# Two mLSTM/attention layers and a compressed-attention layer: a hand-written order of VectorE and ScalarE work before the head loops

## What is computed

```python
for l in range(2):
    h = rmsnorm(x, norm_mix_g[l])
    q,k (conv + silu), v, o, gates i,f, attention q,k,v, ga, gb = split(h @ w_in[l])
    logf = log_sigmoid(f + b_fgate); ig = i + b_igate       # 4 heads: gate rows
    hm = mlstm(q, k, v, ig, logf)                            # running sum and running max of the rows
    ha = sliding_window_attention(aq, ak, av)                # 16 query heads, 4 key/value heads
    x = x + (sigmoid(ga) * (hm @ wm) + sigmoid(gb) * (ha @ wa)) @ w_out[l]
    x = x + square(relu(rmsnorm(x) @ w_up)) @ w_down
x = rmsnorm(x, final_g)
h = rms_norm(x, pre_gain)
# third layer: k,v of three branches (compressed, selected, full), q, 3 gates per head, z
kc = silu(blocks(k_cmp) @ w1) @ w2; vc likewise               # "x2": tokens of two strides, then "hidden"
x = x + rms_norm(sum over branches(gate * attention) * z @ w_out)
```

## Time and profile before

| | |
|---|---|
| median of 3 runs | 2405.76 us (2405.76 to 2406.56) |
| the profiled execution | 2405.57 us, its span 2403.5 us |
| TensorE busy | 2317.2 us, 96% of the span |
| VectorE, ScalarE, GpSimd busy | 920.9, 972.0, 885.2 us |
| mean granted clock | 0.982 |
| transfers | 193.84 MB, 81 GB/s |

### The profile page before, as it was taken

One profiled execution on the slowest core, in us unless ns is written; L12 is line 12 of the kernel. 1 busy time (PEld: TensorE's weight loads), 2 busy tenths in 40 slices (PEclk: granted clock), 3 DMA queues, 4 the chain that ended last, 5 costly groups with the idle time before them and its releaser, 6 DMA issues.

```text
span 2403.5 us, 35769 instructions
## 1 busy us (share of the span) xinstructions
PE 2317.2 (96%) x11397; PEld 1917.0 (80%) x11397; DVE 920.9 (38%) x1907; ACT 972.0 (40%) x2051; POOL 885.2 (37%) x672
## 2 busy tenths in 40 slices
PE   6999999999999998999999999999999999999996
PEld 4888888788888886888888788888887878888885
DVE  7343343324132136243343324132136335445452
ACT  4455455434232234455455434222234244445443
POOL 3333333444444444333333444444444321221213
PEclk9999999999999999999999999999999999999998
DMA  3221222222222222221222222222223221110202
GB/s 121 70 77 63 87 70 70 79 87 96 97 97 96 96 91 93 70 79 61 87 71 69 79 89 94 97 97 96 96 89 117 104 71 53 44 64 32 70 35 70
DMA packets 58793, 193.84 MB, mean 81 GB/s; under 512 B 6654, under 2 KB 11311, under 8 KB 58352
## 3 DMA queue, kind: packets, MB, share of 16 engines
q1 hardware_dynamic: 50400, 177.48, 21.7%
q10 hardware_dynamic: 8336, 15.60, 1.9%
HBM read 190.89 MB, written 2.16 MB: 80 GB/s over the span
## 4 chain that ended last, share of the span: by engine, by line
PE 89%; DVE 5%; ACT 2%; issue 2%; ACTq 0%; DVEq 0%; POOL 0%; POOLq 0%
PE ps L485 25%; PE ps L487 24%; PE ps L486 24%; PE ps L547 4%; PE ps L527 3%; PE ps L535 2%; PE ps L645 1%; PE ps L501 1%; PE ps L633 1%; PE ps L786 1%; PE ps L748 1%; PE ps L811 1%; DVE sz L1363 0%; DVE tn L1805 0%; ACT e_buf L908 0%
## 5 line engine op out<-in xcount | busy, mean ns | idle before, releaser
L446 POOL TENSOR_TENSOR w_lo<-w_raw,w_hi 128x512 fp32r<-128x512 f32 x664 | 878.6, 1327 | 1497.4 <-ACT w_hi L861 1493.5
L485 PE MATMUL ps<-hT_hi,w_hi 128*128 128x512 f32 x1600 | 653.6, 409 | 0.6 <-DVE qn L1333 0.6
L487 PE MATMUL ps<-hT_hi,w_lo 128*128 128x512 f32 x1600 | 630.9, 394 | 0.0
L486 PE MATMUL ps<-hT_lo,w_hi 128*128 128x512 f32 x1600 | 630.2, 394 | 0.0
L861 ACT ACTIVATE w_hi<-w_raw 128x512 fp32r<-128x512 f32 x664 | 411.3, 626 | 483.3 <-PE ps L487 455.3
L487 PEld LDWEIGHTS ps<-hT_hi,w_lo 128*128 128x128 f32 x1600 | 304.0, 190 | 66.8
L485 PEld LDWEIGHTS ps<-hT_hi,w_hi 128*128 128x128 f32 x1600 | 305.0, 191 | 64.4 <-issue 8.6
L486 PEld LDWEIGHTS ps<-hT_lo,w_hi 128*128 128x128 f32 x1600 | 305.1, 191 | 56.3 <-issue 0.5
L485 PE MATMUL ps<-u_hi,w_hi 128*128 128x512 f32 x512 | 201.7, 394 | 0.0
L486 PE MATMUL ps<-u_lo,w_hi 128*128 128x512 f32 x512 | 201.7, 394 | 0.0
L487 PE MATMUL ps<-u_hi,w_lo 128*128 128x512 f32 x512 | 201.7, 394 | 0.0
(11 more groups left out here) (289 smaller groups left out, 3326.0 us busy)
## 6 DMA issues: line engine op xcount, KB each, us to landing
w_raw<-w_all SPq DMA_DIRECT2D x332, 512.0 KB, 3.2
bias<-scr_w ACTq DMA_DIRECT2D x8, 512.0 KB, 3.8
biasn<-scr_n ACTq DMA_DIRECT2D x4, 1024.0 KB, 5.2
w1k<-w_in ACTq DMA_DIRECT2D x2, 1024.0 KB, 8.4
w1v<-w_in ACTq DMA_DIRECT2D x1, 2048.0 KB, 15.0
out<-x SPq DMA_DIRECT2D x8, 256.0 KB, 2.0
x<-x_in SPq DMA_DIRECT2D x4, 256.0 KB, 6.3
x<-x_in ACTq DMA_DIRECT2D x4, 256.0 KB, 5.7
```

The costliest lines, as they stand in the source:

```text
L446: nc.gpsimd.tensor_tensor(w_lo[:, h, :], raw[:, h // 2, (h % 2) * HALF:(h % 2 + 1) * HALF], w_hi[:, h, :].bitcast(F32), ALU.subtract).then ...
L485: nc.tensor.matmul(ps[:, p, :], wh, hi[:, kk, :], start=(kk == 0), stop=False)
L486: nc.tensor.matmul(ps[:, p, :], wh, lo[:, kk, :], start=False, stop=False)
L487: last = nc.tensor.matmul(ps[:, p, :], wl, hi[:, kk, :], start=False, stop=(kk == KT - 1))
```

## The change

1. **Order of TensorE.** In layer 1 the gate product comes before k1 and no longer after it. Layer 0 keeps its order.
2. **VectorE in the two layers** no longer walks the list: its stores, tiles and gate rows between the norm and the loop are written out by hand. The gate rows are cut in two (`gate_rows_in` up to what ScalarE needs, `gate_rows` after its Exp and Ln), and tiles and stores stand between and behind them.
3. **ScalarE in the two layers**: the high parts of the tiles are spread over the steps, and tiles 4 to 7 (layer 0) and 6 and 7 (layer 1) come after the step `gatesT`. The copies of the bias tables move from VectorE to ScalarE.
4. **k**: VectorE writes each half once; ScalarE copies it to the other 64 partitions (`keys`), two instructions of 64x512 a unit.
5. **Gate weights**: layer 0's load is issued at the start of the program, before the tables' loads, and its high part is made after the norm. Those of layer 1 and of the third layer are loaded before the MLP and split in its last chunk, by ScalarE after the quarter h0 of the second `up` unit and by VectorE after its store. The buffers of gate weights and gate rows change places.
6. **x2** in the third layer: VectorE writes the scaled product as one 128x512 instruction to `vtmpn`, ScalarE copies from there to `x2` in four instructions of 64x256, with a stride in what it reads. The tiles are made in lots of 3, 3 and 2 behind the first three x2 units.

```diff
-PRE_LATER = unit("k", 0)[:3] + [("norm_",)] + unit("k", 0)[3:] + unit("k", 1) + PRE_TAIL
+PRE_LATER = unit("k", 0)[:3] + [("norm_",)] + unit("k", 0)[3:] + [("gates",)] + unit("k", 1) + PRE_TAIL
...
@@ scalar
+                elif kind == "x2":
+                    act.wait_ge(g_free[u.b], u.m + 2)
+                    for i in range(2):
+                        for odd in range(2):
+                            last = nc.scalar.activation(x2[n // 2][DH * odd:DH * (odd + 1), 2 * (n % 2) + i, :, :],
+                                                        strided_tokens(vtmpn[DH * i:DH * (i + 1), n % 2, :], odd), ACT.Copy)
+                    last.then_inc(x2_done, 1)
+            def keys(n):
+                u = cur["k", n]
+                act.wait_ge(g_free[u.b], u.m + 2)
+                nc.scalar.activation(kdup[DH:P, 2 * n, :], kdup[0:DH, 2 * n, :], ACT.Copy).then_inc(k_copied, 1)
+                nc.scalar.activation(kdup[0:DH, 2 * n + 1, :], kdup[DH:P, 2 * n + 1, :], ACT.Copy).then_inc(k_copied, 1)
+            gate_weights(0, gw_raw)
             for dst, src in ((oh_w[:, :], onehot_w), (tabw[:, :], tab_w), (oh_n[:, :], onehot_n), (tabn[:, :], tab_n)):
                 nc.scalar.dma_start(dst, src).then_inc(tab_in, 16)
...
-                stored()
-                gate_weights(l, gw_raw)
                 ln_exp()
                 for s in PRE[l]:
                     if s[0] == "norm_":
                         norm()
-                        if l > 0:
+                        if l == 0:
                             gate_weights_hi(l, gw_raw, gw)
...
-                        if s == ("h0", "k", 0) and l == 0:
-                            gate_weights_hi(l, gw_raw, gw)
-                        if s == ("u1", "k", 0) and l > 0 or s == ("u1", "k", 1) and l == 0:
-                            hi_parts(l, range(KT // 2))
-                        elif s == ("u1", "v", 1):
+                        if s == ("u1", "k", 0) and l > 0:
+                            keys(0)
+                            hi_parts(l, (0, 1))
+                        elif s == ("u1", "k", 1):
+                            if l == 0:
+                                keys(0)
+                            keys(1)
+                            if l == 0:
+                                hi_parts(l, (0, 1))
+                        elif s == ("u1", "v", 0) and l > 0:
+                            hi_parts(l, (3,))
+                        elif s == ("u1", "v", 0):
+                            tables_out()
+                        elif s == ("h0", "v", 1) and l > 0:
+                            hi_parts(l, (4,))
...
                     elif s[0] == "TK":
...
+                        if s[1] == 0 and l == 0:
+                            hi_parts(l, (3,))
+                        elif s[1] == 1 and l > 0:
+                            hi_parts(l, (5,))
...
                         nc.scalar.activation(grow[:, 4, :], grow[:, 4, :], ACT.Ln, bias=1.0).then_inc(gr_log, 1)
+                        hi_parts(l, (2,))
                     elif s[0] == "gatesT":
...
                                              ACT.Exp, scale=-1.0).then_inc(t_free[t_.b], 1)
+                        hi_parts(l, range(4 if l == 0 else 6, KT))
...
                 stored()
+                gate_weights(l + 1, *((gw_raw,) if l < DEPTH - 1 else (gwn_raw,)))
                 norm()
...
+                    if s == ("h0", "up", 1):
+                        if l < DEPTH - 1:
+                            gate_weights_hi(l + 1, gw_raw, gw)
+                        else:
+                            gate_weights_hi(l + 1, gwn_raw, gwn)
...
                     if s == ("u1", "x2", 0):
-                        hi_parts(DEPTH, range(KT // 2))
+                        hi_parts(DEPTH, range(2))
                     elif s == ("u1", "x2", 1):
-                        hi_parts(DEPTH, range(KT // 2, KT))
+                        hi_parts(DEPTH, range(2, 5))
+                    elif s == ("u1", "x2", 2):
+                        hi_parts(DEPTH, range(5, KT))
@@ vector
                     for i in range(2):
-                        for dst in range(2):
-                            half = slice(DH * i, DH * (i + 1))
-                            last = V.tensor_tensor(kdup[DH * dst:DH * (dst + 1), 2 * n + i, :], ps[half, u.b, :], rs[half, :],
+                        half = slice(DH * i, DH * (i + 1))
+                        last = V.tensor_tensor(kdup[half, 2 * n + i, :], ps[half, u.b, :], rs[half, :], ALU.mult)
...
+                    if n >= 2:
+                        dve.wait_ge(x2_done, n - 1)
+                    V.tensor_tensor(vtmpn[:, n % 2, :], g, rs12, ALU.mult).then_inc(g_free[u.b], 1)
...
+                V.memset(grow[:, 10, :], 1.0)
+                link(V.memset(grow[:, 5, :], 0.0))
                 if l == 0:
                     gate_weights_lo(l, gw_raw, gw)
+                dve.wait_ge(rs_ready, 2 * l + 1)
+                store(("u1", "k", 0), cur["k", 0])
+                if l == 0:
+                    store(("u1", "k", 1), cur["k", 1])
+                tile(l, 0, rs[:, :])
+                tile(l, 1, rs[:, :])
+                tile_lo(l, 0)
+                tile_lo(l, 1)
+                gate_rows_in(pre["gates",][0])
+                tile(l, 2, rs[:, :])
+                if l == 0:
+                    store(("u1", "v", 0), cur["v", 0])
+                else:
+                    store(("u1", "k", 1), cur["k", 1])
+                tile_lo(l, 2)
+                gate_rows()
+                tile(l, 3, rs[:, :])
+                if l == 0:
+                    store(("u1", "v", 1), cur["v", 1])
+                else:
+                    store(("u1", "v", 0), cur["v", 0])
+                tile_lo(l, 3)
+                tile(l, 4, rs[:, :])
+                if l > 0:
+                    store(("u1", "v", 1), cur["v", 1])
+                tile_lo(l, 4)
+                tile(l, 5, rs[:, :])
+                tile(l, 6, rs[:, :])
+                tile_lo(l, 5)
+                tile(l, 7, rs[:, :])
+                tile_lo(l, 6)
+                tile_lo(l, 7)
...
                     if s == ("u1", "x2", 0):
-                        norm_tiles(DEPTH, range(KT // 2), rs12)
-                        gate_weights_lo(DEPTH, gwn_raw, gwn)
+                        tile(DEPTH, 0, rs12)
+                        tile(DEPTH, 1, rs12)
+                        tile_lo(DEPTH, 0)
+                        tile_lo(DEPTH, 1)
+                        tile(DEPTH, 2, rs12)
                     elif s == ("u1", "x2", 1):
-                        norm_tiles(DEPTH, range(KT // 2, KT), rs12)
+                        tile(DEPTH, 3, rs12)
+                        tile_lo(DEPTH, 2)
+                        tile(DEPTH, 4, rs12)
+                        tile_lo(DEPTH, 3)
+                        tile(DEPTH, 5, rs12)
+                        tile_lo(DEPTH, 4)
+                    elif s == ("u1", "x2", 2):
+                        tile(DEPTH, 6, rs12)
+                        tile_lo(DEPTH, 5)
+                        tile(DEPTH, 7, rs12)
+                        tile_lo(DEPTH, 6)
+                        tile_lo(DEPTH, 7)
```

More of the change, by code:

```diff
@@ L101, in place_fill @@
     return out
-PRE_TAIL = [("gates",)] + unit("v", 0) + unit("v", 1) + [("TK", 0), ("TK", 1), ("gatesT",)]
-PRE_FIRST = unit("k", 0) + unit("k", 1)[:3] + [("norm_",)] + unit("k", 1)[3:] + PRE_TAIL
-PRE_LATER = unit("k", 0)[:3] + [("norm_",)] + unit("k", 0)[3:] + unit("k", 1) + PRE_TAIL
+PRE_TAIL = unit("v", 0) + unit("v", 1) + [("TK", 0), ("TK", 1), ("gatesT",)]
+PRE_FIRST = unit("k", 0) + unit("k", 1)[:3] + [("norm_",)] + unit("k", 1)[3:] + [("gates",)] + PRE_TAIL
+PRE_LATER = unit("k", 0)[:3] + [("norm_",)] + unit("k", 0)[3:] + [("gates",)] + unit("k", 1) + PRE_TAIL
 PRE = [PRE_FIRST] + [PRE_LATER] * (DEPTH - 1)
@@ L268, in two_layers_and_nsa @@
         u_hl = [new("u_hi", [P, KT, S], F32R, at=[r32_at]), new("u_lo", [P, KT, S], F32R, at=[r32_at + 16384])]
-        gw_raw = new("gw_raw", [P, KT * P], at=[r32_at])
-        gw = [new("gw_hi", [P, KT * P], F32R, at=[r32_at + 4096]), new("gw_lo", [P, KT * P], F32R, at=[r32_at + 8192])]
+        gw_raw = new("gw_raw", [P, KT * P], at=[scr_at])
+        gw = [new("gw_hi", [P, KT * P], F32R, at=[scr_at + 4096]), new("gw_lo", [P, KT * P], F32R, at=[scr_at + 8192])]
         sig = new("sig", [P, 2, KT, S], at=[sig_at])
@@ L273, in two_layers_and_nsa @@
         hx = [new("hx_hi", [P, KT, S], F32R, at=[sig_at]), new("hx_lo", [P, KT, S], F32R, at=[sig_at + 16384])]
-        grow = new("grow", [MH, 11, S], at=[scr_at])
+        grow = new("grow", [MH, 11, S], at=[r32_at])
         a = [scr_at]
@@ L742, in _ @@
                     pe.wait_ge(x2_pos, 2)
+                    pe.wait_ge(x2_done, 4)
                     for kv in range(2):
@@ L963, in norm, with tables_out @@
                 nc.scalar.activation(rs[:, :], rs[:, :], ACT.Exp, scale=-0.5).then_inc(rs_ready, 1)
+            def keys(n):
```

(43 more changed lines are left out.)

116 lines of the change are left out of this document (30 added, 86 removed).

## The result

The kernel after takes **2386.52 us** (2386.08 to 2387.39), the kernel before, on the same chip, 2405.81 (2405.76 to 2406.56): a ratio of 0.9919, 95% interval 0.9905 to 0.9934. The forecast was 2385.4, its range 2381 to 2392. The profiled execution took 2386.76, its span 2385.0; before, 2405.57 and 2403.5.

The account below looks back on a forecast made before the run. TensorE, busy 96% of the span, was taken as the bound, with holes before the head loops and low clock behind them. Gains of 8.5 + 7.6 + 4.3 = 20.4 us gave 2385.4, range 2381 to 2392.

Parts of the forecast that it names:

- Order of layer 0: Layer 0: gates start 1.1 later, conv 0 8.35 earlier, gate rows 1.25 shorter; 8.5 us gained (6.6 to 9.7).
- the two instructions named: Layer 0, second part of the gate rows: instructions of 1.60 for 0.68 and 1.30 for 0.47 beside GpSimd's splits; 1.25 taken.
- the clock stays up: Rival, chance 0.12: gate-row transposes and conv 0 run at 2.4 GHz in one or both layers; one layer gives 2381.5.
- Layer 1: Layer 1: gates run without a wait, conv 0 starts between 957.9 and 959.9, before 966.18; 7.6 us gained (6.3 to 8.3).
- Third layer: Third layer: k0 starts 5.5 earlier, less 0.8 for ScalarE's copies and 0.4 for table rows; 4.3 us gained (2.0 to 5.5).
- at 0.4 each, ScalarE's list gives tile 7 at 1853.5: Third layer: with strided copies of 0.4 us, tile 7 is ready just before TensorE asks at 1853.9.
- the mark I had set: Third layer's x2 copies: the forecast is wrong if one strided copy takes over 0.64 us.
- The rival of the strided copies: Chance 0.22: third layer's copies take 0.64 or more, tiles 3 us late, gate rows stay at 8.75; 2390.7.
- the rival that ends slower: Chance 0.06: late x2 copies delay next units' weight halves; slower from 2.8 us per copy, 2411 at 3.2.
- The 0.4 for the table rows: Third layer: rows_n, issued after x2 3's copies and the last tile, lands at 1860.3, k0 ending at 1860.1; 0.4 lost.
- Gate weights in the MLP: MLP: splitting gate weights on ScalarE and VectorE fits in VectorE's standing time before up stores; cost 0.
- Waits only move: Rival, chance 0.05: in both layers gate rows still end last and ScalarE's high parts hold the copies; 2404.

Follow-up runs that it names:

- r1: Kernel after, with the third layer's x2 stores and lots of tiles as before (gate weights stay in the MLP): 2383.8 us.
- r2: Kernel after, with x2 stored by VectorE straight from PSUM as before, no ScalarE copies, the new lots of 3, 3 and 2 kept: 2383.05 us.
- r8: Kernel after, with layer 1's gate product behind k1 again, the rest of the order kept: 2394.46 us.
- r3: Kernel before, with the third layer's part alone (gate weights in the MLP, staged x2 copies, new lots): 2405.17 us.
- r5: Kernel after, with layer 0's gate weights loaded on SP's queue and their high part made after the first half of k0: 2384.61 us.
- r10: r9 with 12 more matmuls whose result nobody reads, in layer 0's pause before the transposes of v1: 2375.58 us.
- r9: Kernel after, with r2's x2 stores, r5's gate-weight start, and matmuls whose result nobody reads in layer 1's pauses: 2378.05 us.

## Why the prediction was right, and where it was not

**Order of layer 0: under-sized** (8.5 forecast, 11.1 measured, above the bound of 9.7). The hole went as laid out, and the terms can be read. Start and gates: -1.37 for -1.1, since the added issue took 0.67 us and not 0.40 and the first matmul came 0.68 late; the wait was for `gw_lo`, 3.35, as told. Its low part took 1.68 for 1.22: it waited out the rest of a running split, 0.46, not a whole one as the 1.7 of the prediction's upper value has it. Gate rows: 7.04 for 8.75, so 1.71 where 1.25 was taken. Of the two instructions named the first fell to 0.74 (L1539 after), but the second still took 1.33 (L1541), and the first instruction of the chain grew to 1.77 from 0.68 (L1537) beside a split. The two scans, which I had at 2.2 as their own length, fell to 1.21; that step of the prediction was wrong, and it paid for the rest.

What remains is the clock: the gate-row transposes 2.20 for 3.54 (1.34) and three matmuls fewer at the low level (0.6). 8.35 - 1.37 + 1.71 + 1.34 + 0.6 = 10.6, of 11.1; most of what is left is that the gate-row transposes began 0.56 behind v1's, where 1.0 was laid out. The clock's part is this execution's: r1, r2 and r8 have the same instructions in layer 0 and end conv 0 at 63.18, 62.81 and 63.16, so that the term comes out at 9.8 to 10.2 by them. It is above 8.5 in all four. So the rival "the clock stays up" came true by half, in this layer; I had its price (some 4 us a layer) and took the clock as all or nothing.

**Layer 1: right** (7.6 forecast, 7.1 measured). The wait for the store of v1 was 2.23, that for the copies 0.64, the low clock stayed. r8 shows that nearly all of the term (6.5) rests on the gate product's place. It came out although two gate-row instructions stayed at 1.60 (L1539) and 1.33 (L1541), since here too both scans took 1.21.

**Third layer: wrong** (4.3 forecast, 0.3 measured, below the bound of 2.0). The failed step is "at 0.4 each, ScalarE's list gives tile 7 at 1853.5". The copies took 0.65, and 0.64 was the mark I had set. Tile 7 came at 1840.8; with the 18.4 by which the stage began earlier that is 1859.2, or 5.7 late. Twelve copies at 0.25 more each are 3.0 of it (an estimate); the rest is a step that the list left out, that ScalarE stands for VectorE's stores (3.36 us before the second four copies), while these wait for ScalarE's high parts and GpSimd's splits.

The rival of the strided copies named the wait for the tiles at 2.0 (2.36 and 0.21 measured) but not the one before it: ScalarE's list also holds the weight halves of the fourth x2, and I followed them only for the rival that ends slower. The two waits, 1.60 and 2.57, and the low clock behind them (the gate product at 1.2 GHz) ate the 3.65 of x2 and more. The 0.4 for the table rows didn't come: behind k0 TensorE has no wait that it did not have before. r3 gives this part alone 1.1 us against the kernel before, within its uncertainty nothing; its norm's sum is already 1.1 earlier (1826.17 for 1827.29), and behind k0 it has the 1.5 of the clock that the kernel after has; the stage itself takes 1.2 more. r1 and r2 show that the kernel is 2.7 to 3.5 faster without the copies.

I took the value nearest to a plain row when the only strided row, VectorE's 0.60 for 256 elements, spoke for the other. The Trainium skill, "SBUF — State Buffer", section "Door 1: The DMA port swizzle", charges each access to a new 16-byte line; the reads step 64 bytes, and 0.65 for 256 elements beside 0.63 for 512 plain ones agrees in direction.

**Gate weights in the MLP: right at 0.** VectorE's idle time before the stores of up went from 213.2 to 208.8 and TensorE has no new wait there (it is 18.4 us ahead at the norm's sum of the third layer as at the end of conv 0 in layer 1):

```profile
L1412 DVE SCALAR_TENSOR_TENSOR e_buf<-ps,rs 128x512 f32<-128x512 f32 x64 | 44.3, 692 | 208.8 <-PE ps L487 208.8
```

**"Waits only move" and "slower"** fell in the layers. r8 shows the first one's mechanism, though: there the gate rows come late again and 0.6 us is won.

**Slips in the sums.** The first paragraph puts the fall to 0.50 into the window of 50 to 55 us; the row has 0.76 there, and 0.50 belongs to the windows from 55 to 65. The upper bound of layer 0 adds up to 9.5 by its terms (8.35 + 1.75 - 0.6), not 9.7. "The waits only move" gives 2401.4 by its terms (20.4 less 8 in each layer), 2404 only with the third layer at 2.0 as well. None of them moves the forecast.

So 2385.4 was near 2386.5 because a term too small by 2.6 stood beside one too large by 4.0 and one too large by 0.5: -20.4 forecast, -18.5 measured in the spans. That the errors cancelled was luck, and some 1 us of the first is the clock of one execution.

## What to carry to other kernels

A copy moved to an idle engine is not free when that engine also feeds the bottleneck in program order: write down what stands behind it in its list, and price it by a row with the same access pattern. Where VectorE works beside GpSimd, lay both timelines side by side; a duration in the trace may be that of the instruction plus its neighbour's. And where small waits decide if TensorE's clock falls, expect little lateness ahead of a hole to come out larger behind it (0.7 us became 3.55 here). Read what a small change gives at the end of its own stage, against the same point of the other kernel: of two runs that came out 1.9 and 2.5 us faster in the whole (r5, r10 against r9), neither was ahead there.
